# Expert loop of a diffusion backbone: one-hots made two pairs ahead, results stored in feature order and read with a step

## The reference

```
scores = sigmoid(x @ w_router)                       # 64 experts; 6 per token, from 4 of 8 groups
combine[token, e] = normalised weight of e for this token, or 0
hid    = silu(x @ w_gate[e]) * (x @ w_up[e])          # 256 wide, for each expert e
routed = sum_e (hid * combine[:, e]) @ w_down[e]      # back to 1024 features
out    = routed + (silu(x @ ws_gate) * (x @ ws_up)) @ ws_down
```

## Time and profile before

| | us |
|---|---|
| median of 3 runs | 1752.52 |
| lowest and highest run | 1752.44, 1754.31 |
| span of the profiled execution | 1752.8 |
| PE busy in it | 1607.8 (92%) |
| ACT busy in it | 698.3 (40%) |
| DVE busy in it | 518.0 (30%) |

### The profile page before, as it was taken

How to read it: one execution, slowest core, us unless ns; L and a number is a source line. 1 busy time by engine, 2 the same in 40 slices (tenths; PEclk the granted TensorE clock), 3 DMA queues, 4 the chain that set the end, 5 groups by cost and what they waited for, 6 DMA issues and landing times.

```text
span 1752.8 us, 30448 instructions
## 1 busy us (share of the span) xinstructions
PE 1607.8 (92%) x13039; PEld 1131.2 (65%) x13039; DVE 518.0 (30%) x857; ACT 698.3 (40%) x1055; POOL 18.6 (1%) x25
## 2 busy tenths in 40 slices
PE   5999999989999999999997998999999999999995
PEld 3767766856666666666665776866666666666663
DVE  1034044151222223232323216232222223232324
ACT  2213322233454545454544204225454545454444
POOL 0000000010000000000000000010000000000000
PEclk8999888989999999999998999899999999999998
DMA  9967566546999999999998333438999999999970
GB/s 315 323 227 266 193 251 240 204 168 272 354 370 357 366 358 365 359 358 367 354 370 301 87 118 156 186 126 320 356 368 359 354 365 363 364 358 366 353 286 25
DMA packets 130113, 510.50 MB, mean 291 GB/s; under 512 B 11257, under 2 KB 19601, under 8 KB 97297
## 3 DMA queue, kind: packets, MB, share of 16 engines
q1 hardware_dynamic: 124832, 506.23, 75.9%
q10 hardware_dynamic: 5232, 3.57, 0.7%
HBM read 506.64 MB, written 3.15 MB: 291 GB/s over the span
## 4 chain that ended last, share of the span: by engine, by line
PE 58%; ACT 23%; DVE 12%; issue 5%; DMA 1%; DVEq 1%; ACTq 0%
PE psum L1230 57%; ACT arena L503 22%; DVE arena L1121 8%; DVE arena L1032 1%; PE psum L1551 1%; DMA arena<-in_moe_router_bias 1%; DVE arena L803 0%; DVE arena L1126 0%; ACT arena L526 0%; DVE arena L845 0%; ACTq L500 0%; DVEq L1134 0%; ACT arena L744 0%; ACT L514 0%; PE psum L1698 0%
## 5 line engine op out<-in xcount | busy, mean ns | idle before, releaser
L1230 PE MATMUL psum<-arena 128*64 128x256 f32 (+9 forms) x12756 | 1577.3, 348 | 112.9 <-DVE arena L1032 63.7
L1230 PEld LDWEIGHTS psum<-arena 128*64 128x64 f32 (+3 forms) x12756 | 1100.9, 136 | 582.4 <-issue 347.1
L503 ACT ACTIVATE arena<-psum 128x512 f32<-128x512 f32 (+4 forms) x514 | 455.7, 903 | 573.8 <-PE psum L1230 468.0
L1121 DVE TENSOR_TENSOR arena<-psum,arena 128x512 f32<-128x512 f32 x128 | 137.7, 1076 | 523.8 <-ACT arena L503 523.8
L503 ACT ACTIVATE arena<-arena 128x512 bf16<-128x512 f32 (+1 forms) x144 | 88.6, 625 | 148.8 <-DVE arena L1121 146.2
L1126 DVE TENSOR_TENSOR arena<-arena 128x512 bf16<-128x512 f32 x128 | 88.7, 693 | 101.1 <-ACT arena L503 101.1
L1105 DVE COPY arena<-psum 128x512 f32<-128x512 f32 x64 | 44.3, 693 | 182.4 <-PE psum L1230 182.4
L825 DVE TENSOR_TENSOR arena<-psum,arena 128x16 f32<-128x16 f32 x12 | 2.1, 175 | 144.4 <-PE psum L1230 144.4
L510 ACT ACTIVATE arena<-arena 128x512 f32<-128x512 f32 x20 | 12.3, 629 | 73.6 <-DVE arena L845 73.6
L845 DVE SCALAR_TENSOR_TENSOR arena<-psum,arena 128x128 f32<-128x128 f32 x64 | 17.8, 343 | 65.6 <-PE psum L1230 65.6
L676 ACT ACTIVATE arena<-psum 128x256 f32<-128x256 f32 x64 | 24.7, 386 | 30.0 <-PE psum L1230 30.0
(11 more groups left out here) (137 smaller groups left out, 309.6 us busy)
## 6 DMA issues: line engine op xcount, KB each, us to landing
arena<-in_moe_w_gate SPq DMA_DIRECT2D x64, 2048.0 KB, 7.9
arena<-in_moe_w_up SPq DMA_DIRECT2D x64, 2048.0 KB, 12.6
arena<-in_moe_w_down SPq DMA_DIRECT2D x64, 2048.0 KB, 9.3
arena<-in_ada_w SPq DMA_DIRECT2D x24, 2048.0 KB, 15.1
arena<-in_hgrn_w_in SPq DMA_DIRECT2D x10, 2048.0 KB, 13.5
arena<-in_na_w_qkv SPq DMA_DIRECT2D x6, 2048.0 KB, 18.1
arena<-in_hgrn_w_out SPq DMA_DIRECT2D x1, 4096.0 KB, 12.6
arena<-in_na_w_o SPq DMA_DIRECT2D x1, 4096.0 KB, 13.7
```

The lines of the kernel that those rows point to most:

```text
L503: return act.activation(out, in_, ACT.Copy, **kw)
L1121: dve.tensor_tensor(y_rest[:, :, ps].rearrange("s k p -> s p k"), psum[:, 6 + half, :].rearrange("s (p k) -> s p k", k=K), y[:, j, 0, :, p ...
L1230: return pe.matmul(out, lhsT, rhs, start=start, stop=stop, skip_group_check=True, **kw)
```

## The change

Two things are changed in the expert loop. First, DVE makes the one-hot matrix of pair n+2 in the step of pair n, after `hid` and after the copy of the gathered bank; the matrix of pair 1 is made ahead of the loop. Second, `y` and `y_rest` hold the 1024 features in their plain order, so ACT and DVE go through result and output straight, and the combine loads its 128 weight columns with a step of eight elements (`k::K`).

```diff
-        y = sc(3 * D, (2, 3, K, P), BF16)
+        y = sc(3 * D, (2, 3, D), BF16)
-        y_rest = route.rearrange("p n a e -> p (n a e)")[:, 0:D].rearrange("p (k t) -> p k t", k=K)
+        y_rest = route.rearrange("p n a e -> p (n a e)")[:, 0:D]
 # ACT, pair_step
-                    copy(y[:, j, 0, :, half * (P // 2):(half + 1) * (P // 2)].rearrange("s k p -> s p k"),
-                         psum[:, 6 + half, :].rearrange("s (p k) -> s p k", k=K)).then_inc(M.y_high, 1)
-                    ps = slice(half * (P // 2), (half + 1) * (P // 2))
+                    ds = slice(half * BLOCK, (half + 1) * BLOCK)
+                    copy(y[:, j, 0, ds], psum[:, 6 + half, :]).then_inc(M.y_high, 1)
                     act.wait_ge(M.y_rest, n * 2 + (half + 3))
-                    copy(y[:, j, 1, :, ps], y_rest[:, :, ps]).then_inc(M.y_mid, 1)
+                    copy(y[:, j, 1, ds], y_rest[:, ds]).then_inc(M.y_mid, 1)
 # DVE
-            def pair_step(M, r, n, j, next_expert):
-
-                if next_expert is not None:
-
-                    one_hots(M, r, next_expert, 1 - j)
+            def pair_step(M, r, n, j, later_expert, last=False):
+
                 dve.wait_ge(M.silu, n + 1)
                 dve.wait_ge(M.hot_t, n + 1)
                 dve.scalar_tensor_tensor(out=hid[:, j], ...).then_inc(M.hid, 1)
-                if next_expert is not None:
+                if not last:
                     gathered(M, n + 1, 1 - j)
+                if later_expert is not None:
+                    one_hots(M, r, later_expert, j)
                 for half in range(2):
                     dve.wait_ge(M.y_high, n * 2 + (half + 1))
-                    dve.tensor_tensor(y_rest[:, :, ps].rearrange("s k p -> s p k"), ...)
+                    dve.tensor_tensor(y_rest[:, ds], psum[:, 6 + half, :], y[:, j, 0, ds], ALU.subtract)\
+                       .then_inc(M.y_rest, 1)
                     ...
 # DVE, experts_pass
+                one_hots(M, r, 2, 1)
                 gathered(M, r * PAIRS, 0)
-                pair_step(M, r, r * PAIRS, 0, 2)
-                with dve.Fori(0, PAIRS // 2 - 1) as h:
+                pair_step(M, r, r * PAIRS, 0, 4)
+                with dve.Fori(0, PAIRS // 2 - 2) as h:
                     for i in (1, 2):
-                        pair_step(M, r, r * PAIRS + h * 2 + i, i % 2, h * 4 + 2 * (i + 1))
-                pair_step(M, r, r * PAIRS + PAIRS - 1, 1, None)
+                        pair_step(M, r, r * PAIRS + h * 2 + i, i % 2, h * 4 + 2 * (i + 2))
+                pair_step(M, r, r * PAIRS + PAIRS - 3, 1, E - 2)
+                pair_step(M, r, r * PAIRS + PAIRS - 2, 0, None)
+                pair_step(M, r, r * PAIRS + PAIRS - 1, 1, None, last=True)
 # PE, combine
-                        ins = mm(psum[:, k // 2, (k % 2) * NT:(k % 2 + 1) * NT], y[:, j, part, k],
+                        ins = mm(psum[:, k // 2, (k % 2) * NT:(k % 2 + 1) * NT], y[:, j, part, k::K],
```

More of the change, by code:

```diff
@@ L157, in build @@
         h_rest = xg
-        y_rest = route.rearrange("p n a e -> p (n a e)")[:, 0:D].rearrange("p (k t) -> p k t", k=K)
+        y_rest = route.rearrange("p n a e -> p (n a e)")[:, 0:D]
         sq = cut(K * NT, (K, NT), at=scratch_at)
-        sh_room = y[:, 0].rearrange("p i k t -> p (i k t)").bitcast(F32).rearrange("p (n a f) -> p n a f", n=3, a=2)
+        sh_room = y[:, 0].rearrange("p i d -> p (i d)").bitcast(F32).rearrange("p (n a f) -> p n a f", n=3, a=2)
         sh_silu, sh_hid, sh_hidT = (sh_room[:, n] for n in range(3))
@@ L1115, in pair_step @@
                                          in1=psum[:, 4, F:2 * F], op0=ALU.mult, op1=ALU.mult).then_inc(M.hid, 1)
-                if next_expert is not None:
+                if not last:
                     gathered(M, n + 1, 1 - j)
+                if later_expert is not None:
+                    one_hots(M, r, later_expert, j)
                 for half in range(2):
                     dve.wait_ge(M.y_high, n * 2 + (half + 1))
[L1120 to L1123, removed]
+                    ds = slice(half * BLOCK, (half + 1) * BLOCK)
+                    dve.tensor_tensor(y_rest[:, ds], psum[:, 6 + half, :], y[:, j, 0, ds], ALU.subtract)\
+                       .then_inc(M.y_rest, 1)
                     dve.wait_ge(M.y_rest, n * 2 + (half + 3))
                     dve.wait_ge(M.y_mid, n * 2 + (half + 1))
-                    ins = dve.tensor_tensor(y[:, j, 2, :, ps], y_rest[:, :, ps], y[:, j, 1, :, ps], ALU.subtract)
+                    ins = dve.tensor_tensor(y[:, j, 2, ds], y_rest[:, ds], y[:, j, 1, ds], ALU.subtract)
                 ins.then_inc(M.y_low, 1)
```

## The result

The changed kernel takes 1678.38 us, the median of four runs (1677.65 to 1678.47), beside 1752.48 for the kernel before in the same session: a ratio of 0.9574, with a 95% interval of 0.956 to 0.9587. The profiled execution spans 1676.7 us, 76.2 less than before. The predicted 1677 is within what a measurement can tell.

| stretch | before, us | after, us | difference | predicted |
|---|---|---|---|---|
| up to the first silu | 400.2 | 399.2 | -1.0 | 0 |
| 31 periods of the first layer | 544.4 | 510.8 | -33.6 | -33.6 |
| last silu of it to first of the second | 226.6 | 223.8 | -2.8 | -4.2 |
| 31 periods of the second layer | 544.5 | 510.8 | -33.7 | -33.6 |
| from the last silu on | 37.2 | 32.2 | -5.0 | -4.2 |

The account below looks back on a forecast made before the run. PE was taken to set the loop's pace, with one hole of 1.06 us a pair. From the profiled span, 1752.8 - 67.2 (hole) - 8.4 (split at layer ends) = 1677.2, so 1677 us; range 1664 to 1706.

Parts of the forecast that it names:

- The hole: PE's wait for one_hots before a gather in the loop; closing it gains 1.12 us, times 60 = 67.2 us.
- The rival in which another wait stands there: At the gather another wait stands at the same time; only the layers' ends gain, 1744 us; chance 0.05.
- The moved one-hots at nothing: One_hots on DVE, behind the copy of the gathered bank, costs nothing; if all exposed, 27 us.
- The load with a step: Combine's 1536 bf16 weight loads, columns 16 bytes apart: hidden under matmuls, cost 0; upper bound 200 us.
- both rivals with slow loads: Combine's stepped loads outlast their matmuls: 0.120 us each, 1694 us, chance 0.24; or 0.239 us each, 1877 us, chance 0.11.
- The split: ACT and DVE's rounding and subtraction of the result: 9.1 us becomes 4.9 at a layer's end, gaining 8.4 us in all.
- DMAs at nothing: Weight loads in the loop: the same 6.3 MB in a 16.28 us period stays hidden, cost nothing.

Follow-up runs that it names:

- the kernel with neighbouring columns: Changed kernel with the combine loading 128 neighbouring columns of the plain layout, without a step; features come out in another order: 1678.46 us, 0.9557.
- The experiment with two parts: Changed kernel with the third bf16 part left out of gather and combine, 16 and 8 matmuls fewer a pair: 1580.87 us, 0.901.

## Why the prediction was right, point by point

- **The hole.** Sized right: 1.12 us a pair was forecast, 17.409 - 16.287 = 1.12 came, and PEld's idle of 0.39 us is what remains. Its 67.2 us were 67.3 in the table. The rival in which another wait stands there (1744 us) is out.
- **What closes it.** Here a step of the reasoning failed, though not the sum: it gave the whole hole to the moved one-hots and said of the faster split, "In the loop that is worth nothing of its own". The layout alone closes the hole as well. The split's end at 701.42 was read as 3.4 us of cover for the combine; it was also what one_hots, the instruction queued behind it on DVE, had to wait for. The two parts overlap, and the loop's gain belongs to whichever is made first.
- **The moved one-hots at nothing.** Right; nothing waits for them. `hid` needs cover, forecast as the gather's 2.87 us less about 1; measured, it has 1.5 to 1.6.
- **The load with a step.** The bound taken, 0, was right, and both rivals with slow loads (1694 and 1877 us) are out: 0.061 us a load, under the 0.120 of the one and the 0.239 of the other, and under the 0.109 of a matmul. But the working put the load's columns at 0.04 us from the float32 loads' factor of 2.15; the record grew by 44 ns where that factor gives some 20 (1.15 times 0.02). The cover was wide enough for the miss. Carried to the gather, whose matmuls take 0.055, it would have given no cost where there are 0.26 us a pair.
- **The split.** 4.9 us to the combine were forecast; 4.90 came in the second layer and 5.36 in the first. The split's own 4.84 us agree with the added durations. The rest in the first layer is the 0.52 us by which PE starts late: its way through register read and branch ends 3.68 us behind its last matmul, which the 7.4 us of waiting covered before. So the term was 3.75 us in the first layer and 4.21 in the second, 8.0 instead of 8.4 in all. The two stretches behind the loops gained 7.8 together, but not by this term alone. In the second layer the combine's first 3 us ran at a granted clock of 0.55 before and of 1.00 now, and the stretch gained 0.8 more than the term. In the first layer 3.8 us of gain were there right behind the residual, and 1.0 of them was gone by the next silu, in code that the change doesn't touch. The 1.0 us gained before the first silu lies in such code too; the first silu comes at 396.4 to 400.9 us in the profiles of the kernels with three parts. So it is in part luck that the sum is only 1.4 us off.
- **DMAs at nothing.** Right, with landing times 2 us longer. The experiment with two parts puts the next bound at 15.08 us a pair.

## What to carry to other kernels

Before a gain is put down to a moved instruction, ask why it was late: here it stood behind a slow one, and making that one faster was enough, so each part of a change is priced alone and then with the other in place. The price of an access pattern moves to where it is hidden: the step left ACT and DVE, where it cost 1.8 and 0.4 us an instruction with someone waiting, for weight loads under matmuls that are longer than they are. A wait that shrinks uncovers what stood behind it, so the next late instruction, here a branch at the end of one layer, belongs into the sum.

## What the runs showed of the hardware that was not expected

- The record of a bf16 weight load of 128 columns grows with its step in small grades, 98, 99, 103, 113, 125 and 144 ns for steps of 1, 2, 3, 4, 6 and 8 elements, and no further (142 and 146 ns for 12 and 16). From 64 pieces of 16 bytes to 128 that is (144 - 113) / 64 = 0.5 ns a piece.
- At the end of the first layer a branch over unused code kept PE from work that was ready for 1.94 us with no semaphore in between; without the branch it started 0.05 us behind its releaser. The same branch at the end of the second layer held nothing (0.06 us). Why it does so in one place alone the runs leave open.
- After an idle of 3.68 us the last combine of the first layer ran at a granted clock of 0.51, near the lower level of 1.2 GHz; after 3.23 us that of the second layer ran at 1.00, the upper level of 2.4 GHz. With the same 3.23 us of idle, the kernel with neighbouring columns had 0.50 there for 2.98 us. So the length of the idle alone does not decide; what does the runs leave open.
- With its queues full the DMA side moved 417 GB/s over a whole pair, at a share of 1.02, and each pair's weights then landed later than the last one's, up to 22.3 us, before PE waited for any.
